# Hybrid decoder step, PEER layer: VectorE sums the gates of equal expert choices, and GpSimd scatters whole gates without accumulating

## The reference, cut to what matters

```python
top_s, top_i = lax.top_k(s, PEER_TOPK)                       # 16 of 128 keys, both halves, 8 heads
...
best_s, best_j = lax.top_k(cand_s, PEER_TOPK)                # 16 of the 256 pairs
expert = jnp.take_along_axis(cand_i, best_j, axis=-1)        # of 16384 experts
gate = jax.nn.softmax(best_s, axis=-1)
...
h = jax.nn.gelu(jnp.einsum('nd,nhkd->nhk', xb, u_tab[eb], preferred_element_type=f32), approximate=False)
return jnp.einsum('nhk,nhkd->nd', (gb * h).astype(xb.dtype), v_tab[eb])
```

## Time and profile before

| | us |
|---|---|
| runs | 3292.15, 3283.61, 3290.49 |
| median | 3290.49 |
| the profiled execution | 3288.63 |
| its span, first to last instruction | 3286.9 |
| busy in the span: PE / DVE / ACT / POOL | 2840.2 / 1799.9 / 964.8 / 738.5 |
| the PEER layer's first half, from its first weights | 1526.8 to 2528.1 |
| scatter of gates on POOL, first and last start | 1915.7 to 2557.4 |
| the second half's first product on PE | 2568.25 |

### The profile page before, as it was taken

How to read it: one execution, slowest core, us unless ns; L and a number is a source line. 1 busy time by engine, 2 the same in 40 slices (tenths; PEclk the granted TensorE clock), 3 DMA queues, 4 the chain that set the end, 5 groups by cost and what they waited for, 6 DMA issues and landing times.

```text
span 3286.9 us, 45123 instructions
## 1 busy us (share of the span) xinstructions
PE 2840.2 (86%) x17548; PEld 2443.9 (74%) x17548; DVE 1799.9 (55%) x2555; ACT 964.8 (29%) x1148; POOL 738.5 (22%) x630
## 2 busy tenths in 40 slices
PE   3999965778889987496999998888896799999998
PEld 2999953556656665395999998887896688887886
DVE  3455531398764443244578864444453566666555
ACT  1445520002211111122222333232231344444443
POOL 0100003110002222000000067787887100000000
PEclk7999987768889999698999999999998899999999
DMA  3355444123225553232445578787786788887664
GB/s 133 130 182 183 172 140 119 50 68 96 42 79 148 160 158 118 106 141 93 168 170 172 185 233 231 229 243 223 236 253 177 290 317 299 310 283 244 243 243 175
DMA packets 245312, 594.93 MB, mean 181 GB/s; under 512 B 76345, under 2 KB 180162, under 8 KB 192658
## 3 DMA queue, kind: packets, MB, share of 16 engines
q1 hardware_dynamic: 173874, 484.95, 43.6%
q0 software_dynamic: 54592, 90.41, 10.4%
q10 hardware_dynamic: 16640, 16.78, 1.5%
HBM read 535.05 MB, written 56.97 MB: 180 GB/s over the span
## 4 chain that ended last, share of the span: by engine, by line
PE 28%; POOL 16%; issue 5%; DVE 3%; DMA 2%; ACT 0%; DVEq 0%; SPq 0%; POOLq 0%
POOL expert_gates L2124 14%; PE px_bank L272 8%; PE px_bank L274 8%; PE px_bank L273 8%; PE px_bank L2171 4%; POOL px_fetch L2135 2%; DMA expert_gates<-px_chosen,px_spot 1%; DVE px_w_r L2319 1%; DMA px_parts<-sample_parts 0%; DVE ps_topi L2333 0%; PE px_bank L2180 0%; DMA px_w<-in_peer_v 0%; DVE ps_top L2330 0%; DMA px_w<-in_peer_wq 0%; DVE px_rows L2499 0%
## 5 line engine op out<-in xcount | busy, mean ns | idle before, releaser
L2319 DVE TENSOR_TENSOR px_w_r<-px_w,px_wh 128x2048 fp32r<-128x2048 f32 x256 | 583.6, 2290 | 250.7 <-ACT px_wh L2246 249.4
L2246 ACT ACTIVATE px_wh<-px_w 128x2048 fp32r<-128x2048 f32 x256 | 489.7, 1913 | 636.3 <-PE px_bank L274 261.1
L272 PE MATMUL px_bank<-px_high,px_wh 128*128 128x256 f32 x2048 | 596.1, 291 | 87.9 <-DVE px_w_r L2319 87.8
L273 PE MATMUL px_bank<-px_low,px_wh 128*128 128x256 f32 x2048 | 589.6, 288 | 0.0
L274 PE MATMUL px_bank<-px_high,px_w_r 128*128 128x256 f32 x2048 | 589.5, 288 | 0.0
L2124 POOL DMA_INDIRECT expert_gates<-px_chosen,px_spot x256 | 478.6, 1870 | 102.5 <-issue 76.2
L272 PEld LDWEIGHTS px_bank<-px_high,px_wh 128*128 128x128 f32 x2048 | 403.6, 197 | 94.5 <-DVE px_w_r L2319 94.5
L272 PE MATMUL px_bank<-px_wh,px_gh 128*128 128x512 f32 x1024 | 400.2, 391 | 43.3 <-issue 40.2
L273 PEld LDWEIGHTS px_bank<-px_low,px_wh 128*128 128x128 f32 x2048 | 403.5, 197 | 0.0
L274 PEld LDWEIGHTS px_bank<-px_high,px_w_r 128*128 128x128 f32 x2048 | 402.9, 197 | 0.0
L274 PE MATMUL px_bank<-px_wh,px_gl 128*128 128x512 f32 x1024 | 399.8, 390 | 0.0
(11 more groups left out here) (392 smaller groups left out, 4305.5 us busy)
## 6 DMA issues: line engine op xcount, KB each, us to landing
px_w<-in_peer_u SPq DMA_DIRECT2D x128, 1024.0 KB, 5.2
px_w<-in_peer_v SPq DMA_DIRECT2D x128, 1024.0 KB, 4.9
pj_w<-in_w_in SPq DMA_DIRECT2D x49, 1024.0 KB, 5.0
expert_gates<-rh_empty ACTq DMA_DIRECT2D x16, 1024.0 KB, 6.7
at_values<-in_kv_pages POOLq DMA_DIRECT2D x128, 128.0 KB, 2.8
at_pages<-in_kv_pages SPq DMA_DIRECT2D x128, 128.0 KB, 2.2
out_w<-in_w_o SPq DMA_DIRECT2D x16, 1024.0 KB, 4.8
px_w<-in_peer_wq SPq DMA_DIRECT2D x16, 1024.0 KB, 4.8
```

The lines of the kernel that those rows point to most:

```text
L272: pe.matmul(out, w_high, high, start=start, stop=False, skip_group_check=True)
L273: pe.matmul(out, w_high, low, start=False, stop=False, skip_group_check=True)
L2246: act.activation(w_high[u % WH][:], w[s][:], ACT.Copy).then_inc(raised, 1)
L2319: v.tensor_tensor(w_low[s][:], w[s][:], w_high[u % WH][:], ALU.subtract).then_inc(lowered, 1)
```

## The change

VectorE makes for each choice `z` of each token the sum of the gates of all choices of the same token with the same place: `total_gate(n)` compares `place[:, t]` with its column `z`, multiplies by the gates and accumulates along the row, so that `whole_gate[:, t, z]` is the whole gate of that expert. Choices that fall on one word now write the same value, and the scatter writes without accumulating. The 256 sums are spread over the turns of tiles 37 to 62, ten in a turn, behind `prepare` and ahead of the sample row. Each scatter waits for its sum (`totaled`). The waits after each 32 scatters stay, and SyncE waits for `totaled` too before it reads the first gates. Nothing else is touched.

```diff
+        whole_gate, junk = sb("whole_gate", [P, 2, P]), [sb(f"junk{s}", [P, P]) for s in range(2)]
...
                         sp.wait_ge(chose, 2)
+                        sp.wait_ge(totaled, 2 * PH * EK)
...
                         pool.wait_ge(scattered, 16 * sent)
+                    pool.wait_ge(totaled, sent + 1)
                     pool.indirect_dma_start(gates_d, bass.IndirectOffsetOnAxis(ap=spot[:, t, z:z + 1], axis=0),
-                                            chosen[:, 2, t, z:z + 1], None, compute_op=ALU.add).then_inc(scattered, 16)
+                                            whole_gate[:, t, z:z + 1], None).then_inc(scattered, 16)
...
+                def total_gate(n):
+
+                    z, t = divmod(n, 2)
+                    if n == 0:
+                        v.wait_ge(chose, 2)
+                    if n >= 2:
+                        v.wait_ge(totaled, n - 1)
+                    v.scalar_tensor_tensor(junk[n % 2][:], place[:, t], place[:, t, z:z + 1], chosen[:, 2, t, :],
+                                           ALU.is_equal, ALU.mult, accum_out=whole_gate[:, t, z:z + 1]) \
+                        .then_inc(totaled, 1)
...
+                    if CHOSEN_AT < u <= CHOSEN_AT + 2 * PH * EK // 10 + 1:
+                        for n in range(10 * (u - CHOSEN_AT - 1), min(10 * (u - CHOSEN_AT), 2 * PH * EK)):
+                            total_gate(n)
```

More of the change, by code:

```diff
@@ L2041, in peer_layer @@
         link, chose, shifted, exped = (cx.sem(f"px_{x}") for x in ("link", "chose", "shifted", "exped"))
-        moved, scattered = cx.sem("px_moved"), cx.sem("px_scattered")
+        moved, scattered, totaled = cx.sem("px_moved"), cx.sem("px_scattered"), cx.sem("px_totaled")
         dotted, curved_s, added = cx.sem("px_dotted"), cx.sem("px_curved_s"), cx.sem("px_added")
```

## The result

| | before | changed |
|---|---|---|
| median of the runs, us | 3289.14 | 3198.22 |
| lowest and highest, us | 3283.61 to 3292.15 | 3189.60 to 3202.90 |
| the profiled execution, us | 3288.63 | 3196.48 |
| its span, us | 3286.9 | 3194.8 |
| POOL / DVE busy, us | 738.5 / 1799.9 | 644.7 / 1867.8 |

The ratio of the runs is 0.9723, 95% interval 0.9702 to 0.9744: faster, by about 91 us where 79 were forecast. The lines are three to fourteen further down than before: the scatter is line 2127, the row fetch 2138, the lowering of the weights 2322, the sums 2408, the sample rows 2443 and 2456.

A forecast was written before the change was run, and what follows sets the result against it. GpSimd's issue rate was taken as the bound from first row fetch to second half: 39 cycles of 12.7 us, plus 30, 4, 35 and 10.8, start it at 2489.4, 79 us earlier, giving 3211 us; 8-in-10 range 3172 to 3294.

The forecast's parts named there:

- cycle, with holds of long instructions and sums: GpSimd's fetch, six scatters, next fetch: 12.7 us in place of 14.7, plus 4 us in all for the sums' holds.
- waits for landing, in all: Six GpSimd waits for landed scatters: 24.5 us beyond the usual gap becomes about 30, since GpSimd arrives earlier.
- fetch 39 to the last scatter: End of GpSimd's stretch: 25 instructions at 1.30 us and 2.5 for two holds, 35 us in place of 45.6.
- The price of the scatter: On GpSimd: 1.00 us without accumulation, taken from the fetch's 0.99, against 1.55 for the accumulating scatter.
- The holds: VectorE's three long two-input instructions per cycle delay GpSimd: 2.7 us packed, 4.8 apart, 3.6 expected.
- 41% of the way between packed and apart: Where the old 14.7 us cycle lay between 13.5 (long VectorE instructions packed) and 16.4 (apart); reused for the new cycle.
- The sums: 256 VectorE instructions after tiles 37 to 62, 0.30 us each, 77 us in all, hidden in its waits for rows.
- second rival: VectorE becomes the bound in tiles 42 to 62: 3241 us at 0.45 per sum, 3271 at 0.60; chance 0.10.
- The first: Rival: GpSimd's scatter stays at 1.55 us, the cycle at 14.7, sums only add holds: 3295 to 3310 us; chance 0.22.
- The third: Rival: TensorE becomes the bound, GpSimd's cycle falls under 11.52 us, 128 us saved: 3163 us; chance 0.12.
- The halfway case under the first rival: GpSimd's scatter at 1.25 us: a cycle of 13.8 and 35 us saved, 3255 us.
- the forecast case: Plain scatter on GpSimd at 0.9 to 1.25 us: 3175 to 3258 us, chance 0.56.

The follow-up runs named there:

- The run without scatters: The changed kernel with VectorE's lowering made from one SBUF input, and in it no scatters and no SyncE wait for them: 3149.43 us, 0.9557 of before.
- With nothing holding GpSimd: The changed kernel with the weights' low part made by a one-input tensor_scalar in place of the two-input tensor_tensor: 3215.94 us, 0.9785 of before.
- with pauses: The one-input lowering kernel in which scatters also wait for VectorE's lowerings, three for each lowered tile: 3188.87 us, 0.9686 of before.

## Why the prediction was right, step by step

| step | forecast | measured |
|---|---|---|
| plain scatter, free, us | 1.00 | 0.97 |
| fetch to fetch, free | 9.1 | 8.96 (2448.19 to 2457.15) |
| one sum on VectorE | 0.30 | 0.273 |
| two tiles with 20 sums | 12.7 | 12.08 |
| cycle, with holds of long instructions and sums | 12.8 | 12.5 |
| waits for landing, in all | 30 | 23.2 |
| fetch 39 starts | 2443.6 | 2426.13 |
| fetch 39 to the last scatter | 35 | 36.1 |
| last scatter to TensorE's first product | 10.8 | 10.6 |
| first product | 2489.4 | 2472.86 |
| TensorE's stall | near 30 | 25.5 |

The measured cycle is 2426.13 less 1915.83 less 23.2, by 39. The measured landing waits are the 23.3 and one more of 1.7, each less the usual 0.30. The forecast's 12.8 is 12.7 and the 4 us for the sums.

**The price of the scatter** was taken from the fetch, the nearest indirect DMA without accumulation, and not from the accumulating scatter itself. That row was the right one: 968 ns, though a fetch moves 128 rows of 8 KB and a scatter 128 words. The run without scatters shows what else the software queue carries:

```profile
q0 software_dynamic: 17728, 90.26, 7.9%
```

So of the 54592 packets before 144 belong to each scatter, and of the 25920 now 32. The prediction's estimate from the Trainium skill, "GPSIMD Engine Reference", section 4, and "DMA: Bandwidth & Descriptors", Rules for kernel authors, was a second list of 128 reads that goes away with the accumulation; the trace agrees on the direction, with 112 packets fewer for each scatter and not 128. What GpSimd does in the 0.58 us no run here shows.

**The holds** came out as modelled. A held scatter now ends some 0.85 us after VectorE's instruction with two SBUF inputs ended, 1.42 before. One place, VectorE and then GpSimd:

```profile
1964.22 2.27 DVE L2322 TENSOR_TENSOR px_w_r<-px_w,px_wh 128x2048 fp32r<-128x2048 f32 x1
```

```profile
1965.45 1.91 POOL L2127 DMA_INDIRECT expert_gates<-px_whole_gate,px_spot  x1 [0.30 <-issue]
```

The lowering ends at 1966.49, the scatter at 1967.36. The probe that the Trainium skill's page "SBUF — State Buffer" reports, by which tensor_tensor would not stall DMAs, doesn't agree with these rows, and the rule beside it does. The prediction used 41% of the way between packed and apart, fitted on the kernel before; 3.5 us of holds in a cycle (12.5 less 8.96) against 3.6 forecast, with 0.1 for the sums. The cycle is 12.6 without the sums and with five in a turn too, so the share hardly depends on where the sums stand; why it is 41%, and that it carries over from one fit, no run explains, and some luck is in it. The sums' own hold is small: the 21 scatters that start during a sum and meet no long instruction take 1.03 to 1.05 us, and not 0.97.

**The sums** were sized at 0.30 and took 0.273: the next one starts while the last accumulator is read.

```profile
1960.10 0.34 DVE L2408 SCALAR_TENSOR_TENSOR px_junk<-ps_hit,px_chosen 128x128 f32<-128x128 f32 x1
1960.37 0.07 DVE L2408 DVE_READ_ACCUMULATOR px_junk<-ps_hit,px_chosen 128x1 f32 x1
1960.37 0.34 DVE L2408 SCALAR_TENSOR_TENSOR px_junk<-ps_hit,px_chosen 128x128 f32<-128x128 f32 x1
```

That they would hide was right, and shown by the kernel without them. The prediction's second rival was nearer than its chance of 0.10 said, though: VectorE was full in tiles 42 to 62, and only because GpSimd needs about as much (without the wait for landing its first ten cycles take 12.5 us on the mean without the sums and 12.1 with them) was there no price. The kernel with the sums made twice shows that rival's mechanism at its size.

**The term that was mis-sized** most is the wait for landing: 30 forecast, since GpSimd would arrive earlier while the landing came no sooner; 23.2 measured. From the fetch to the scatter behind such a wait it was 11.77 at the first one; here it is 10.21 (1975.31 to 1985.52). Over all six it was 60.6 and is 58.4, sooner at four and later at two, so the landing moved little, as assumed. What failed is the earlier arrival: 14 scatters stand between those fetches and the waits, 7.8 us at 0.56 each, but from the fetches to the waits' start GpSimd took 33.4 us in place of 34.2, since VectorE's instructions now held it there too (the fetch at 1975.31 took 1.9 us, the one at 1995.68 1.00). These 7 us and the cycle's 0.3, 12 us over 39 cycles, make the 16.5 by which the first product came earlier than forecast, with 1.1 and 1.5 against them (the end of the stretch, and a first fetch that came later). 3.2 us were lost again behind the stretch, so that the execution is 13 us below the forecast's 3209.6.

**The rivals.** The first (the scatter stays at 1.55) is what the sums with the accumulating scatter show in full: 3290.5, a little less than its 3295 to 3310. The third (TensorE becomes the bound) didn't come: TensorE ran nearly unbroken from 2300 to 2440, but GpSimd's chain had no pause there but one wait for landing, and it still ended last, by 25.5 us. What that rival promised, 3163, was reached only when the landing waits had gone and fourteen fetches had moved behind the last scatter: 3162.1. The halfway case under the first rival is off by its own working: a scatter of 1.25 gives 10.6 free and 3.0 of holds, a cycle of 13.6 and not 13.8, and some 42 us saved and not 35. Only the upper end of the forecast case, 3258, rests on that.

## What to carry to other kernels

When GpSimd's DMA issue sets the pace, count its instructions and price each kind by a row of the same trace: dropping the accumulation from a scatter gave 0.58 us each where nothing held it, 0.45 on the mean of all, at the price of work on an engine that was waiting anyway. A wait that guards the order of writes should look as far back as the order of work can be made to allow, since it costs the landing of all that was issued in between, here some 20 us. And before an engine is freed of what holds it, ask who profits from its pauses.

## What the hardware showed that was not expected

- With nothing holding GpSimd, its row of indirect DMAs (one each 1.27 us) stopped TensorE in the middle of tiles, 78 times for 48.6 us, and the granted clock fell to 0.50 after such a stop. Without scatters there were none of these stops (150.00 of 150.00 us busy), with pauses 41 for 20.0 us. In both kernels compared, where VectorE's holds break up the row, no such stop of 0.15 us or more is in the traces; that the holds keep it away is argued from that, and why the row stops TensorE stays open.
- Taking load from VectorE (five sums in a turn) didn't speed GpSimd up: the first five cycles went from at most 12.1 to between 13.0 and 14.2 us in the one profile of each, and the mean of 39 stayed, 12.6 after 12.5.
